# Reordering VectorE's opening: pooled tiles, filter decays and row sums of the modulation

## The reference, cut to what matters

```python
# modulation: six vectors of 1024 out of c
mod_x = silu(c) @ mod_w[0] + mod_b[0]
sh1, sc1, g1, sh2, sc2, g2 = split(mod_x, 6)
hx = x * (1.0 + sc1) + sh1
# pooling over windows 2, 4, 8, 16, four channel groups
p  = stack([centred_window_mean(hx_g, w) - hx_g for g, w in groups])
y  = einsum('blgc,gcd->blgd', p, w_group) * scale
x  = layer_norm(ALPHA * x + g1 * y, ln_g, ln_b)
# Hyena's filters: spectra of filters that only the second layer needs
h  = sin_mlp(features) @ fw_out
h  = h.reshape(512, 2, 2, 1024) * exp(-t * deltas)      # "decay"
k_f = rfft(two_sided_kernel(...))
```

## Time and profile before

| | |
|---|---|
| median of 3 runs | 1775.94 us (1773.77 to 1776.53) |
| profiled execution, own time | 1777.26 us |
| its span in the profile | 1775.9 us |
| TensorE busy | 98% of the span |
| VectorE busy | 53% |
| ScalarE, GpSimd busy | 36%, 42% |
| mean granted clock of TensorE | 0.991 |

### The profile page before, as it was taken

One profiled execution on the slowest core, in us unless ns is written; L12 is line 12 of the kernel. 1 busy time (PEld: TensorE's weight loads), 2 busy tenths in 40 slices (PEclk: granted clock), 3 DMA queues, 4 the chain that ended last, 5 costly groups with the idle time before them and its releaser, 6 DMA issues.

```text
span 1775.9 us, 20931 instructions
## 1 busy us (share of the span) xinstructions
PE 1732.5 (98%) x8260; PEld 1411.6 (79%) x8260; DVE 941.6 (53%) x1473; ACT 637.8 (36%) x970; POOL 744.9 (42%) x382
## 2 busy tenths in 40 slices
PE   8989999999999999999999999999999999999997
PEld 4547888888897667888888888888888988888887
DVE  8789543321275765744444223588786754444125
ACT  2533222221255564443333223532333633333122
POOL 0213444444463022544444445565453634444442
PEclk9989999999999999999999999999999999999999
DMA  9864852222221021223222223422223223222222
GB/s 371 318 244 143 273 176 99 102 96 95 96 88 60 10 71 36 72 89 101 95 95 95 95 95 107 179 94 95 83 96 107 96 83 101 101 95 95 95 95 83
DMA packets 59792, 205.28 MB, mean 116 GB/s; under 512 B 6764, under 2 KB 10030, under 8 KB 57774
## 3 DMA queue, kind: packets, MB, share of 16 engines
q1 hardware_dynamic: 57965, 197.81, 32.2%
q10 hardware_dynamic: 1730, 6.14, 0.9%
HBM read 188.19 MB, written 15.73 MB: 115 GB/s over the span
## 4 chain that ended last, share of the span: by engine, by line
PE 81%; DVE 9%; POOL 3%; ACT 2%; issue 2%; DMA 2%; SPq 0%; DVEq 0%; ACTq 0%; POOLq 0%
PE ps L609 24%; PE ps L611 24%; PE ps L610 24%; PE ps L641 3%; PE ps L646 1%; DMA w_raw<-in_w_stream 1%; POOL w_lo L1817 1%; DVE mod_ring L1997 1%; PE ps L691 1%; DVE filter_taps L2066 1%; DVE softmax_stats L2491 1%; DMA spectra<-filter_spectra 1%; DVE probs_t_lo L2547 1%; ACT w_hi L1298 1%; PE ps L707 0%
## 5 line engine op out<-in xcount | busy, mean ns | idle before, releaser
L1817 POOL TENSOR_TENSOR w_lo<-w_raw,w_hi 128x1024 fp32r<-128x1024 f32 (+1 forms) x231 | 561.5, 2432 | 809.8 <-ACT w_hi L1298 726.9
L1298 ACT ACTIVATE w_hi<-w_raw 128x1024 fp32r<-128x1024 f32 (+1 forms) x231 | 243.8, 1056 | 772.5 <-PE ps L611 722.0
L609 PE MATMUL ps<-act_hi,w_hi 128*128 128x512 f32 x1240 | 485.7, 392 | 8.0 <-DVE x_residual L2088 4.8
L611 PE MATMUL ps<-act_hi,w_lo 128*128 128x512 f32 x1240 | 482.2, 389 | 0.0
L610 PE MATMUL ps<-act_lo,w_hi 128*128 128x512 f32 x1240 | 482.1, 389 | 0.0
L609 PEld LDWEIGHTS ps<-act_hi,w_hi 128*128 128x128 f32 x1240 | 233.8, 189 | 58.1 <-DVE x_residual L2088 5.7
L611 PEld LDWEIGHTS ps<-act_hi,w_lo 128*128 128x128 f32 x1240 | 233.5, 188 | 48.4
L610 PEld LDWEIGHTS ps<-act_lo,w_hi 128*128 128x128 f32 x1240 | 233.8, 189 | 48.0 <-issue 0.7
L609 PE MATMUL ps<-f_hidden_hi,w_hi 128*128 128x512 f32 (+1 forms) x546 | 206.2, 378 | 0.2 <-POOL w_lo L1817 0.2
L611 PE MATMUL ps<-f_hidden_hi,w_lo 128*128 128x512 f32 (+1 forms) x546 | 204.8, 375 | 0.0
L610 PE MATMUL ps<-f_hidden_lo,w_hi 128*128 128x512 f32 (+1 forms) x546 | 203.3, 372 | 0.0
(11 more groups left out here) (348 smaller groups left out, 2716.6 us busy)
## 6 DMA issues: line engine op xcount, KB each, us to landing
w_raw<-in_w_stream SPq DMA_DIRECT2D x250, 512.0 KB, 3.2
mod_ring<-in_mod_t SPq DMA_DIRECT2D x18, 512.0 KB, 8.1
x_tokens<-in_mod_t SPq DMA_DIRECT2D x18, 512.0 KB, 10.0
hy_filter<-spectra SPq DMA_DIRECT2D x8, 1024.0 KB, 4.8
mod_ring_more<-in_mod_t SPq DMA_DIRECT2D x12, 512.0 KB, 8.6
spectra<-filter_spectra SPq DMA_DIRECT2D x12, 512.0 KB, 9.8
filter_spectra<-spectra SPq DMA_DIRECT2D x12, 512.0 KB, 5.2
spectra<-filter_spectra SPq DMA_DIRECT2D x20, 256.0 KB, 5.8
```

What stands on the lines that cost most here:

```text
L609: PE.matmul(o, lh, rh, start=start, stop=False, **kw)
L611: return PE.matmul(o, ll, rh, start=False, stop=stop, **kw)
L1298: SC.activation(B.weights(c)[0][:, 0:n], B.WR[:, c % 2, 0:n], ACT.Copy).then_inc(S.w_hi, 1)
L1817: GP.tensor_tensor(low[:, 0:n], B.WR[:, c % 2, 0:n], f32(high[:, 0:n]), ALU.subtract).then_inc(S.w_lo, 1)
```

## The change

Only the order of VectorE's instructions in the opening moves, and one wait of GpSimd. No operation is added or left out.

```diff
@@ GpSimd, start()
-        GP.wait_ge(S.mod_used, 31)
+        GP.wait_ge(S.decayed, 25)
         w_lo(2)
@@ VectorE, start()
         decays(3)
-        mod_tiles(16, 20)
+        mod_tiles(16, 21)
+        decays(4)
         for k in range(KD):
             difference(k)
-            if k % 2:
-                if k == 1:
-                    VE.wait_ge(S.decay_in[1], 16)
-                    VE.wait_ge(S.spectrum, 6)
-                decay_tile(4, k // 2)
-        mod_tiles(20, 24)
+        mod_tiles(21, 24)
         decays(5)
-        mod_tiles(24, 29)
+        mod_tiles(24, 26)
         pooled_tile(0)
         pooled_tile(1)
         pooled_tile(2)
         running_sum(1)
         pooled_tile(3)
         running_sum(2)
-        mod_tiles(29, 31)
+        mod_tiles(26, 27)
         for k in range(4, KD):
...
         running_sum(3)
         decays(6)
-        mod_tiles(31, 33)
+        mod_tiles(27, 29)
         pooled_tile(4)
...
         running_sum(7)
-        mod_tiles(33, 35)
-        decays(7)
+        mod_tiles(29, 31)
         VE.wait_ge(S.ln_mean, 1)
         for k in range(KD):
             VE.tensor_tensor(X[:, k, :], X[:, k, :], ps[:, 7, :], ALU.subtract).then_inc(S.ln_centred, 1)
+        decays(7)
         for k in range(1, KD):
...
-        mod_tiles(35, 36)
+        mod_tiles(31, 36)
         VE.wait_ge(S.ln_turned, 1)
```

## The result

The changed kernel takes 1780.12 us (median of 20 runs, 1776.81 to 1784.03) where the kernel before, on the same chip, takes 1774.57 us (20 runs, 1772.21 to 1777.81). The ratio is 1.0031 with a 95% interval of 1.0026 to 1.0037: 5.5 us slower. By its size that is the rival "slower by over 0.2%", not the forecast of +2.1 us; the time lies inside the range.

A forecast was written before the change was run, and what follows sets the result against it. TensorE is busy 98% of the span; VectorE, arriving last, sets the network's start at 140.76. First scaling at W + 19.3, less 139.15, with W = 121.95, gives +2.1 us: 1775.94 + 2.1 = 1778.1 us, range 1774.8 to 1781.6.

The forecast's parts named there:

- slower by over 0.2%: Rival: spectra or tiles arrive more slowly, chunk 4 at 122.8, +4.0 us; over 3.55 us counts; chance 0.24.
- W: Time when chunk 4's high part is ready on ScalarE, predicted 121.95 us; the change is W - 119.85 us.
- The queue decides, and the squares stand behind chunk 4's high part.: SyncE's queue sends chunk 4 at 113.0 instead of 108.14; its high part on ScalarE holds the squares.
- The queue's timing: SyncE's transfers after the gap land at 113.8, 117.0, 118.3, 119.6, and chunk 4 at 120.9 us.
- The squares that it gates come in time.: TensorE's transform behind the copy runs at the low clock, yet its squares don't delay VectorE's additions: no cost.
- W + 7.75: End of VectorE's seven additions of squares: start at W + 2.5, 5.25 us long.
- Everything behind the additions: Five row sums on VectorE take 5.8 us, hiding TensorE's column sums; first scaling 5.74 us after the epsilon.
- Unit 4's decays: On VectorE ahead of the differences, inside 5.03 us of waiting: end at 66.6, free with 0.2 us of cover.
- Pooled tiles ahead of row sums: TensorE's four pooled tiles run through, 6.5 us less, 1.9 given back; pool_linear(1) at 102.0, mean at 112.0.
- pipelining: Reason given for putting the norm's mean out at 112.0 us, after 102.0 + 9.6 + 0.9.
- The lock on SBUF: VectorE instructions with two SBUF inputs and GpSimd exclude each other; without this the sum would be 0.8 us lower.
- The sum made against one execution: Change worked out against the profiled 1777.26 us execution (first scaling 139.15), then added to the median, 1775.94 us.

The follow-up runs named there:

- the first experiment: Changed kernel with chunk 4 fetched ahead of tiles 38 and 39 and spectrum 5 on SyncE's queue: 1775.32 us, ratio 1.0009.
- the kernels with unit 4's part: Kernel before with row sum 20 and unit 4's decays ahead of the differences: 1772.71 us; with GpSimd's low part of chunk 2 also waiting for decay 25: 1771.22 us.

## Where the prediction was right and where it was wrong, step by step

The mechanism that was forecast is the one that ran, but its price was not: +2.1 us forecast, 5.5 measured. That 1780.12 us still lies inside 1774.8 to 1781.6 owes something to luck. The range stands on the median of three runs, 1775.94, which was 1.4 us above that of the twenty later ones; on 1774.57 it would have ended at 1780.3. And "slower by over 0.2%" came true by its number, not by its mechanism: it was to decide from W = 123.4 on, and W was 122.89, which is +3.0 us by the prediction's own formula. The rest has other sources, below.

- *The queue decides, and the squares stand behind chunk 4's high part.* Right in mechanism. The release of the high part is "DMA" at 121.83, predicted 120.9, and the first experiment shows that the queue's order costs 3.9 us.
- *The queue's timing, the first term of the sum that was mis-sized.* The first issue went out at 109.80 (predicted 110.6) and chunk 4 at 112.64 (113.0), each a bit early, but the five transfers took 11.9 us from the first issue instead of 10.3. The second landed 3.8 us behind the first and not 3.2; the third, a half of the spectrum, 2.3 us behind that, where I took 1.3 from the earlier trace rows; the last two, 1.4 and 1.2 apart, are as I had them. W was 122.89, predicted 121.95: +0.9 us. An estimate by the Trainium skill (DMA: Bandwidth & Descriptors, on the anatomy of one DMA), which gives about 2.0 us and then the bytes at 436 GB/s for a DMA that GpSimd issues, would be 8.0 us for the five; these were issued by SyncE, and the trace has 11.9.
- *"The squares that it gates come in time."* Wrong. The transform at the low clock brought the copy at 127.24 and the squares behind it late, and VectorE waited 0.93 us, a term that the sum had at nothing; W + 7.75 for the end of the additions was W + 8.5. This and the step before make the scaling 1.6 us later than forecast (142.85 for 141.25).
- *Everything behind the additions.* Right to 0.1 us: five row sums took 5.73 (5.8), the epsilon had no idle time in front, the scaling came 5.73 later (5.74), TensorE's column sums were hidden.
- *Unit 4's decays.* They began at 64.81 behind their DMA (I had 64.2) and ended at 67.2, so the differences start 0.4 us later than in the earlier trace rows, past the 66.9 that I had named as a limit. It cost less than it gave: this part alone won 2.5 us, more than the 1.15 us of a row sum, because TensorE's shorter wait left its clock up.
- *Pooled tiles ahead of row sums.* The pooled tiles gave what they should and a bit more: no wait from 84 to 90, pool_linear(1) at 100.43 (102.0), since chunk 2's high part ran at 95.70 and not at 97.0. The mean at 109.71 was over a microsecond ahead of the 111 to 112 I had, and it bought nothing, as VectorE's row sums 29 and 30 are the bound there and the queue goes by them. (The prediction's own terms, 102.0 + 9.6 + 0.9, give 112.5 and not the 112.0 that it went on with; no run shows the 0.5 us of "pipelining".)
- *The lock on SBUF.* Splits at 92.62 in 2.49 us: with GpSimd's new wait its low part ran at 96.91, behind them, and held row sum 27 instead (2.32 us at 98.02), as the act splits held row sum 22 (2.29 us at 76.97). The first addition's 1.43 us is the lock again, until GpSimd's end at 125.3. The Trainium skill (SBUF — State Buffer, on its two separate sides) has it so for a GpSimd instruction that reads SBUF, as these do, and the trace agrees with it at both places. GpSimd's two rows, in the timeline of the changed kernel:

```profile
...
96.91 2.35 POOL L1817 TENSOR_TENSOR w_lo<-w_raw,w_hi 128x1024 fp32r<-128x1024 f32 x1 [18.72 <-DVE filter_taps L2066]
...
122.97 2.35 POOL L1817 TENSOR_TENSOR w_lo_extra<-w_raw,w_hi_extra 128x1024 fp32r<-128x1024 f32 x1 [9.00 <-ACT w_hi_extra L1298]
...
```

- *The sum made against one execution, which failed by about as much.* 140.76 and 139.15 came from an execution whose own time, 1777.26 us, was 2.7 us above the median of 20 later ones. Its pooling behind the wait ran at clock 0.50, and its column sums too, while three other executions with this order have the network at 138.44, 138.55 and 139.90. I carried the change, not the level, over to the median, so this went in whole: against 139.4, the mean of the four, the same working would have read +3.5 us and with the 1.6 us above +5.1; against the 138.5 of the first two, +4.4 and +6.0. The 5.5 measured lies between. How long the low clock lasts differs from execution to execution, and I priced it as a constant of the kernel before, with the 0.88 us that VectorE waited for the column sums.

What isn't settled: the time behind the network's start isn't constant. Own time less the network's start is 1634.5 us in the changed kernel's profile and between 1633.0 and 1636.8 in the others, with no order by edit that I can see. A single profiled execution can't place a change better than that. Why the queue's rate fell twice within these 12 us, and whether writes and reads differ in it, was not tried.

## What to carry to other kernels

Before moving work later on an engine, list every transfer that waits for the buffers this work frees, and what the consumer of the last of them stands in front of: here row sums 29 and 30, placed 10.7 us later on VectorE (108.55, against 97.86 before), cost 4 us through a queue and an in-order engine two steps away. When two waits meet at one instruction, undoing one alone says nothing against it; try both together. Take two or three profiled executions of the kernel before making a sum against one, above all when a stretch at the low clock is in the bill: here four of the same order differed by 2.3 us.

## What the runs showed of the hardware

- Five transfers of 512 KB that go out over 2.8 us on an idle queue landed 3.2, 7.0, 9.3, 10.7 and 11.9 us after the first issue, 220 GB/s on average, against 406 GB/s in the earlier trace rows. The rate was not even: 70 to 187 GB/s from 112.5 to 114.2 us, 386 to 468 from 115 to 116.7. From the first issue to chunk 4's high part it was 11.3 to 12.0 us in all five executions with this queue order in which the high part waited for the transfer.
- The mean clock of the same 5.2 us behind a wait of 3.7 to 3.9 us in the same kernel was 0.50 in one execution and 0.68 and 0.70 in two others; behind 2.16 and 2.67 us (the kernels with unit 4's part) it was 1.00. Behind the same wait of 3.13 us the column sums of line 796 took 1.84 us in one execution and 1.02 in two others.
- GpSimd's passes over SBUF lengthened VectorE's additions (3.08 to 5.19 us for four), splits (2.49 to 4.64) and row sums (1.22 to 2.32), and left the decays, which read one operand from PSUM, at 2.47 us.
